# Two transformer blocks on one core: the program begins with the residual input, and four later pieces of its hand-written order are moved

## What is computed

```python
x = first_block(x, mem, ...)      # stage A: mlstm heads + memory attention (4 heads, 256 memory tokens), ffn
                                  # stage B: band attention (12 heads) + memory attention, ffn, rmsnorm
x = second_block(x, ...)          # stage C: 4 differential heads + 8 forgetting heads, ffn, rmsnorm

h = rmsnorm(x, norm_mix_g[0])
q, k, v, o, gates, q_mem = split(h @ a_w_in)          # q, k: causal conv over 4 tokens, then silu
mk, mv = split(mem @ mem_w_kv[0])                     # mem does not depend on x
mem_out = softmax(q_mem @ mk.T / 8) @ mv
x = x + concat([mix_out, mem_out]) @ w_out            # in each stage; then the ffn
...
od = rmsnorm_2(p @ v, subln_g) * 0.8                  # differential heads of stage C
```

## Time and profile before

| | |
|---|---|
| median of 3 runs | 1838.75 us |
| profiled execution, its own time | 1836.94 us |
| its span, first to last instruction | 1835.2 us |
| PE busy | 1815.8 us, 99% |
| DVE, ACT, POOL busy | 935.6, 726.6, 272.4 us |
| granted TensorE clock | 0.997 of full |
| moved by DMA | 173.43 MB, 95 GB/s on average |

### The profile page before, as it was taken

One profiled execution on the slowest core, in us unless ns is written; L12 is line 12 of the kernel. 1 busy time (PEld: TensorE's weight loads), 2 busy tenths in 40 slices (PEclk: granted clock), 3 DMA queues, 4 the chain that ended last, 5 costly groups with the idle time before them and its releaser, 6 DMA issues.

```text
span 1835.2 us, 21592 instructions
## 1 busy us (share of the span) xinstructions
PE 1815.8 (99%) x8853; PEld 1482.8 (81%) x8853; DVE 935.6 (51%) x1445; ACT 726.6 (40%) x1159; POOL 272.4 (15%) x241
## 2 busy tenths in 40 slices
PE   9999999999999999999999999999999999999998
PEld 7877788888888887787888888888876788888886
DVE  6877455442444456546543354458666443323324
ACT  5644444331332435654433133333566332222223
POOL 2001322210121200002221022003001222101210
PEclk9999999999999999999999999999999999999999
DMA  6121123222222332212222222232131223222221
GB/s 241 69 94 56 69 92 115 92 92 95 89 102 88 124 135 92 81 46 93 97 110 92 98 99 97 75 127 91 60 104 51 76 92 109 98 92 92 97 92 63
DMA packets 32338, 173.43 MB, mean 95 GB/s; under 512 B 4064, under 2 KB 6240, under 8 KB 14320
## 3 DMA queue, kind: packets, MB, share of 16 engines
q1 hardware_dynamic: 26848, 162.55, 24.7%
q10 hardware_dynamic: 5392, 9.51, 1.7%
HBM read 169.38 MB, written 2.13 MB: 93 GB/s over the span
## 4 chain that ended last, share of the span: by engine, by line
PE 93%; DVE 3%; ACT 2%; issue 0%; DMA 0%; POOL 0%; SPq 0%; ACTq 0%; DVEq 0%; POOLq 0%
PE ps L964 53%; PE ps L1239 19%; PE ps L898 7%; PE ps L983 6%; PE ps L1088 2%; PE ps L1133 2%; PE ps L1113 2%; DVE WL L1740 1%; PE ps L1172 1%; PE ps L1153 1%; DMA raw<-in_wall 0%; ACT PC L1476 0%; ACT WH L1315 0%; DVE hL L1708 0%; PE ps L878 0%
## 5 line engine op out<-in xcount | busy, mean ns | idle before, releaser
L964 PE MATMUL ps<-hH,WH 128*128 128x512 f32 x1456 | 571.4, 392 | 0.1
L964 PE MATMUL ps<-hH,WL 128*128 128x512 f32 x1456 | 566.8, 389 | 0.0
L964 PE MATMUL ps<-hL,WH 128*128 128x512 f32 x1456 | 566.7, 389 | 0.0
L1740 DVE TENSOR_TENSOR WL<-raw,WH 128x1024 fp32r<-128x1024 f32 (+2 forms) x308 | 377.3, 1264 | 352.0 <-ACT WH L1315 352.0
L1315 ACT ACTIVATE WH<-raw 128x1024 fp32r<-128x1024 f32 (+2 forms) x308 | 301.3, 1026 | 291.5 <-PE ps L1239 228.6
L964 PEld LDWEIGHTS ps<-hH,WH 128*128 128x128 f32 x1456 | 273.3, 188 | 64.4 <-issue 7.5
L964 PEld LDWEIGHTS ps<-hL,WH 128*128 128x128 f32 x1456 | 273.4, 188 | 57.4 <-issue 1.2
L964 PEld LDWEIGHTS ps<-hH,WL 128*128 128x128 f32 x1456 | 273.3, 188 | 57.1
L1239 PE MATMUL ps<-fL,WH 128*128 128x512 f32 x531 | 205.9, 388 | 0.0
L1239 PE MATMUL ps<-fH,WH 128*128 128x512 f32 x531 | 205.9, 388 | 0.0
L1239 PE MATMUL ps<-fH,WL 128*128 128x512 f32 x531 | 205.9, 388 | 0.0
(11 more groups left out here) (364 smaller groups left out, 1965.8 us busy)
## 6 DMA issues: line engine op xcount, KB each, us to landing
raw<-in_wall SPq DMA_DIRECT2D x140, 1024.0 KB, 4.6
raw<-in_wall SPq DMA_DIRECT2D x12, 768.0 KB, 4.0
bias<-in_bias ACTq DMA_DIRECT2D x12, 256.0 KB, 3.0
X<-in_xt SPq DMA_DIRECT2D x8, 256.0 KB, 9.1
CB<-rows ACTq DMA_DIRECT2D x8, 256.0 KB, 3.3
raw<-in_wall SPq DMA_DIRECT2D x4, 256.0 KB, 5.8
mrA<-in_memt ACTq DMA_DIRECT2D x4, 256.0 KB, 6.2
Mb<-m_rows ACTq DMA_DIRECT2D x4, 256.0 KB, 4.7
```

The lines of the kernel that those rows point to most:

```text
L964: mm = e.matmul(ps[b][:, 0:N], ww[:, k, c:c + 128], x[:, k, 0:N], start=(k == 0 and i == 0), stop=(k == 7 and i == 2))
L1740: e.tensor_tensor(WL[n % NCV][:, c], raw[n % NRAW][:, c], WH[n % NCV][:, c].bitcast(F32), ALU.subtract).then_inc(*mark("wl", n, x))
```

## The change

Five edits to the order, and nothing in what is computed:

1. **The start.** The unit of the memory's queries (3080 in `a_w_in`) becomes unit 0, the two memory units 1 and 2. X is loaded by ACT's queue as its first eight instructions (before: by SP, behind unit 1), the memory by SP behind unit 1 (before: by ACT); the constants K come behind them. `qm_first` takes the place of `mk_first`: 48 matmuls of 512 columns for 48 of 256, and keeps its two banks (`hold`) until the spread of the norm's factor. `mkA`, `mvA` and the gate products follow. The squares stand ahead of the memory's products and so ahead of the conversion of unit 3 (q), which stood ahead of them. The norm's two PE steps come after the first and the second tile of q (before: after the queries' second tile and the first tile of q), and one tile more (k, first) stands ahead of the first scores; every later step of stage A stands one tile later against the products.
2. **Drains at the first Rsb.** The gate's drain comes behind those of the queries; before it came first.
3. **Seventh parts.** `out_mid` runs for all four open tiles before the first `out_rest`, in stages A, B and C.
4. **The inverse.** `od_all` keeps DVE's reciprocal alone and stands right behind `probs` of pair 6; ACT's root is the new step `od_root` at the old place.
5. **The store** of four tiles of the first half is cut in two.

```diff
-    u = [("mem_w_kv", 0, 0, 8, 0, 256), ("mem_w_kv", 0, 0, 8, 256, 256)]
-    u += [("a_w_in", 0, 0, 8, 3080, 256)]
+    u = [("a_w_in", 0, 0, 8, 3080, 256)]
+    u += [("mem_w_kv", 0, 0, 8, 0, 256), ("mem_w_kv", 0, 0, 8, 256, 256)]
...
-STORES = ((0, 0, 2), (0, 2, 2), (0, 4, 4), (1, 0, 4), (1, 4, 2), (1, 6, 2))
+STORES = ((0, 0, 2), (0, 2, 2), (0, 4, 2), (0, 6, 2), (1, 0, 4), (1, 4, 2), (1, 6, 2))
...
-        for x in (0, 1):
+        for x in range(4):
             put("out_mid", stage, x, *opened[x])
...
-    for x in range(4):
-        put("conv", 0, x)
-        put("mem_part", "A", x)
-    now["conv"] = 1
-    take()
-    put("mk_first", 0)
+    for k in range(8):
+        if k % 2 == 0:
+            put("conv", 0, k // 2)
+        put("scaled", "mix0", k, None)
+    now["conv"], now["unit"] = 1, 1
+    put("qm_first", 0)
     done.add(0)
-    for m in range(2):
-        tile_done("mkcp", "mkA", m)
+    put("conv", 1, 0)
+    put("mem_part", "A", 0)
+    put("mem_part", "A", 1)
+    put("conv", 1, 1)
+    put("mem_part", "A", 2)
+    put("mem_part", "A", 3)
+    now["conv"] = 2
     put("gate_weights", "A")
-    for k in range(8):
-        put("scaled", "mix0", k, None)
-    tm(1, "memA", "mvA", "mvcp", ntt=2)
-    conv_ahead(4)
+    conv_ahead(3)
     for k in range(8):
         put("square", "s", k, "dve", "pool" if k % 2 else "act")
-    rstd("mix0", 60)
+    fm(1, "memA", "mkA", "mkcp", N=256)
+    tm(1, "memA", "mvA", "mvcp", ntt=2)
+    conv_ahead(5)
     put("gate_products", "A")
-    waiting.append(("gate",))
-    fm(1, "mix0", "qmA", "R")
+    norms.extend([("rstd_first", "mix0", 60), ("rstd_second", "mix0")])
+    waiting.extend([("R", "qmA", 0), ("R", "qmA", 1), ("gate",)])
...
-    fill(gens, 1)
+    fill(gens, 2)
...
-    after_values = {(5, 1): [("od_two",)], (6, 0): [("od_all",)], (6, 1): [("od_mask",)],
+    after_values = {(5, 1): [("od_two",)], (6, 0): [("od_root",)], (6, 1): [("od_mask",)],
...
+    def inverse(p):
+        if p == 6:
+            put("od_all")
...
+                    if a[0] == "mix0":
+                        turns.extend([BANK[("qmA", 0)], BANK[("qmA", 1)]])
...
-                        out_part(stage, b, n, c, seq[7 if m < 2 else early:], ("out", stage, m))
+                        out_part(stage, b, n, c, seq[7:], ("out", stage, m))
...
-                    src = memt.rearrange("p (k t) -> p k t", k=8)
-                    for i in range(4):
-                        e.dma_start(mrA[:, 2 * i:2 * i + 2, :], src[:, 2 * i:2 * i + 2, :]).then_inc(s_mem[i], 16)
+                    src = xt.rearrange("p (k t) -> p k t", k=8)
+                    for k in range(8):
+                        e.dma_start(X[:, k, :], src[:, k, :]).then_inc(s_x[k], 16)
```

More of the change, by code:

```diff
@@ L268, in mem_kv, with soft @@
         tm(1, "mem" + name, "mv" + name, "mvcp", ntt=2)
-    def soft(stage, gens, per, before=None, between=None):
+    def soft(stage, gens, per, before=None, between=None, after_probs=None):
         us = SOFT[stage]
@@ L286, in soft @@
                     put("probs", stage, p, x)
+            if after_probs:
+                after_probs(p)
             if early:
@@ L523, in order @@
     soft("C", gens, lambda p: {4: (1, 0), 5: (1, 0), 6: (1, 0), 7: (1, 0), 8: (1, 1), 9: (1, 1)}.get(p, (1, 1)),
-         None, between_C)
+         None, between_C, inverse)
     out_rest("C", "n2")
@@ L908, in tensor @@
                         e.matmul(ps[b][:, 0:256], diag[:, 0:128], diag[:, 0:256], start=True, stop=True)
-                elif what == "mk_first":
+                elif what == "qm_first":
                     n = a[0]
@@ L915, in tensor @@
                     W = [x[0][:, :].rearrange("p (k c) -> p k c", k=8) for x in (WH, WL)]
-                    bs = [bank(("mkA", m), ("mkv", "mkA", m))[0] for m in (0, 1)]
+                    bs = [bank(("qmA", m), ("linR", "qmA", m), hold=True)[0] for m in (0, 1)]
                     for k in range(8):
-                        if k in (2, 4, 6):
+                        if k == 2:
                             mm = e.matmul(ps[idle][:, 0:256], diag[:, 0:128], diag[:, 0:256], start=True, stop=True)
-                        if k == 6:
                             mm.then_inc(*mark("warmed"))
                         w.wait_ge(*at(*weights_at(n, k)))
-                        for x in act_at("memA", k):
+                        for x in normed("mix0", k):
                             w.wait_ge(*at(*x))
                         for m in (0, 1):
-                            for i, (ww, x) in enumerate(((W[0], mHA), (W[0], mLA), (W[1], mHA))):
-                                mm = e.matmul(ps[bs[m]][:, 0:256], ww[:, k, 128 * m:128 * m + 128], x[:, k, :],
+                            for i, (ww, x) in enumerate(((W[0], hH), (W[0], hL), (W[1], hH))):
+                                mm = e.matmul(ps[bs[m]][:, :], ww[:, k, 128 * m:128 * m + 128], x[:, k, :],
                                               start=(k == 0 and i == 0), stop=(k == 7 and i == 2))
                             if k == 7:
-                                mm.then_inc(*mark("lin", "mkA", m))
-                    FREED[n] = ("lin", "mkA", 1)
+                                mm.then_inc(*mark("lin", "qmA", m))
+                    FREED[n] = ("lin", "qmA", 1)
                 elif what == "gate_products":
@@ L1677, in scalar @@
                         *mark("odc", hd))
-                elif what == "od_all":
+                elif what == "od_root":
                     w.wait_ge(*at("odD", "r"))
@@ L1755, in vector @@
                         w.wait_ge(s_cols if ev.sems else None, 16)
-                        w.wait_ge(s_K if ev.sems else None, 16)
                         w.wait_ge(s_x[k] if ev.sems else None, 16)
@@ L1769, in vector @@
                     w.wait_ge(*at("rsq", a[0]))
+                    w.wait_ge(s_K if ev.sems else None, 16)
                     for x in RCOL_USED[a[0]]:
@@ L2382, in sync @@
                 e.dma_start(raw[0][:, 512 * x:512 * x + 512], wall[:, 512 * x:512 * x + 512]).then_inc(s_first[x], 16)
-            e.dma_start(cols[:, :], colsd).then_inc(s_cols, 16)
+                if x == 0:
+                    e.dma_start(cols[:, :], colsd).then_inc(s_cols, 16)
+            load(1)
+            src = memt.rearrange("p (k t) -> p k t", k=8)
+            for i in range(4):
+                e.dma_start(mrA[:, 2 * i:2 * i + 2, :], src[:, 2 * i:2 * i + 2, :]).then_inc(s_mem[i], 16)
             e.dma_start(K[:, :, :], consts.rearrange("p (i c) -> p i c", i=5)).then_inc(s_K, 16)
@@ L2386, in sync @@
             e.dma_start(graw[:, :, :], gatew[:, 0:64].rearrange("p (k c) -> p k c", k=8)).then_inc(s_gw, 16)
[L2387 to L2390, removed]
             for n in range(2, len(UNITS)):
```

## The result

The changed kernel takes 1846.58 us in the median (5 runs, 1843.04 to 1848.32) against 1837.82 us (5 runs, 1837.62 to 1839.1) for the kernel before: ratio 1.0044, interval 1.0033 to 1.0054. It is 8.8 us slower; 1843.0 was predicted, as 4.25 us more than the kernel before. The executions also lie 5.3 us apart, where those of before lie 1.5 apart. They follow the granted clock, taken as the mean over an execution: 1843.04 us at 0.998, 1844.92 at 0.996, 1846.58 at 0.995, 1848.18 and 1848.32 at 0.994.

A forecast was written before the change was run, and what follows sets the result against it. PE, busy 1815.8 of 1835.2 us, was taken as the bound. Terms -2.0 + 2.65 + 2.2 - 0.5 + 4.9 - 2.7 - 0.3 = +4.25 gave 1841.2 profiled, 1843.0 against the median; range 1838.0 to 1847.0.

The forecast's parts named there:

- Seventh parts: At `out_all` in A, B, C: mid parts moved ahead leave fewer products covering the conversion chain; PE waits longer, +4.9 us.
- The first k behind the spread: At the first k tile: PE stands still until DVE's queries' drains and `O` free the gates' bank, +2.65 us.
- The start: From launch to stage A's first scores: PE starts at 8.15, DVE's work around the squares decides, point reached earlier, -2.0 us.
- The memory heads' first values: Before the memory heads' values in stage A: DVE's copy PTA is late and PE waits, +2.2 us (0 to +2.9).
- mlstm's norm: At mlstm's norm: PE's 0.5 us wait for `fac` goes as DVE has less ahead, -0.5 us (-0.6 to 0).
- The inverse: Before pair 7's scores: reciprocal moves into DVE's pause, root and copies start earlier, PE's wait falls 3.61 to 0.9, -2.7 us.
- The store: In the last traffic: fuller transfer slices after cutting the four-tile store in two, -0.3 us (-0.5 to +0.1).
- DVE's delay runs on: Rival, stage A after the memory heads' values: drains stay 3 us late, PE waits again at k or v tile; 1846, chance 0.10.

The follow-up runs named there:

- The kernel with its waits filled: The changed kernel with PE multiplying constants, results thrown away, in the waits at the memory's keys, first k tile and `out_all` in A, B, C: 1843.31 us.
- the last experiment: The kernel before with the reciprocal's new place and only the first tile's mid part ahead of the first rest part: 1831.55 us, ratio 0.9966.
- the kernel with PE 4 us earlier: The changed kernel with the gate's drain put ahead of the queries' drains again, as before the change: 1846.18 us.

## Why the prediction was right and wrong

The direction was right, and the time lay in the stated range, 0.4 us below its upper end of 1847.0; it lay above the forecast's own range, which ended at 1845.0. The median is 3.6 us above the 1843.0, but the change itself was sized at half: +4.25 us forecast, +8.8 measured. That the times are only 3.6 apart and the changes 4.5 comes from the base: 1838.75 us was the median of three executions of before, and five give 1837.82. The kernel with its waits filled, which shows about what the change costs when the clock doesn't fall, takes 1843.31 us. That looks like the sum, but it is luck in part, since terms in it were off both ways:

- **Seventh parts** (+4.9): the waits are 2.31, 2.23 and 2.22 us where 2.35 was worked out for each, and the chain through add, hH, square and conversion is what binds. Shown by the edit alone and, in the other direction, by the last experiment. As a size the term failed: alone it costs 9.5 us, since each wait of 2.2 us can be followed by half clock that costs 1.6 us.
- **The first k behind the spread** (+2.65): 2.69 measured, and 1.48 with `O` first, where 1.45 was worked out. Another 1.65 us of half clock followed in the profile.
- **The start** (-2.0): wrong. The failed step is that the memory's keys and values follow the queries at 19.4 with no wait, and that what decides on DVE is only the work around the squares. PE began at 8.88, not 8.15, because hH and hL of the first tile stand ahead of it, ended the queries at 20.5, and waited 1.76 us for the memory's low part. I had counted DVE's work for the squares, and not the 6 us in which it does unit 1 and the memory behind X. The first tile of q started at 37.55, not 33.75. The wait of 0.85 at the first q tile, forecast for that work, didn't come since PE was later. At full clock the start is worth 0.0, with half clock behind the wait +1.8. (The sum to the gates' end has a slip: 19.4 + 5.7 + 5.7 + 1.9 is 32.7, not 32.9; the 33.75 doesn't hang on it.)
- **The memory heads' first values** (+2.2): 0.54. DVE's copy was late as worked out: with the first drain at 51.65 instead of 47.9 the sum's 104.95 becomes 108.7, and the values start at 108.86. PE's own time was off, by what the start and the clock had cost it. In the kernel with PE 4 us earlier the wait was 3.33. What is lost ahead of this point on PE counts little, as long as DVE is behind.
- **mlstm's norm** (-0.5): the wait of 0.5 us is gone; laid side by side the traces give -0.7.
- **The inverse** (-2.7): -5.3 alone. The wait fell to 0.30 us, not 0.9 (3.3 us), and the half clock behind it, 1.4 us, went. The wait is shorter than the 0.9 left over in the sum because ACT's copies PTC follow the root at once, 0.53 us behind its start (1404.24 and 1404.77); in before they began 1.12 us behind it (1392.83 and 1393.95), with two issues of transfers (1.07 us) from 1392.83 on, which in the changed kernel run from 1401.91, ahead of the root. The place and the table load's 1.28 us behaved as the row said. The further drain that the Trainium skill ("ScalarE: Activation LUTs", the section on what ACT_TABLE_LOAD costs) adds to a load isn't seen: the load starts at 1402.94 right behind ACT's previous instruction, and the root follows at 1404.24.
- **The store** (-0.3): not to be told from nothing.
- **Not in the sum at all**: 0.9 us in A's open tiles, which comes with the start: there DVE has four steps of the heads ahead of the low part that PE waits for.
- **The rivals**: 1846, the price of "DVE's delay runs on", is nearest to the median, but its sign isn't there. From PTA to the open output tiles at 238 PE waits nowhere 0.1 us or more.

So one mechanism was missing from the whole, the term that the prediction put at nothing: that PE's standing still has a second price behind it. It was in the trace of before, in the 3.42 us that twelve scores take in the earlier trace rows, a row that was quoted but read for its wait only. The parts measured alone add up to 9.5 - 5.3 + 6.4 + 0.8 = +11.4 against +8.8 for all. One reason for the difference can be seen: three of the four parts were measured in kernels that keep the wait before pair 7's scores, and the profiled executions of two of them have 6.8 us of half clock there, while the changed kernel has neither the wait nor that. The rest is within what the half clock does or doesn't do from one execution to the next; I can't assign it closer.

## What to carry to other kernels

When PE is busy 99% of the time, price a new wait of 2 us on it as a range from 2 to nearly 4, and a removed one too: look in the rows behind the old waits for products that take longer than their fellows, and in the spread of the executions for how often. When an order is changed to cover one wait, count the products that are left between the last thing the conversion chain waits for and its user; moving products ahead of the chain's start takes cover away one for one (here six products, 1.4 us, and three, 0.7 us, the other way). Before crediting an earlier PE, ask which engine sets the next meeting point: here DVE's copy at 108 us took back what PE had won.

## What the runs showed of the hardware

In the ten traces the granted clock, outside the first microseconds and the tail, left its upper level only around the end of a wait of PE. How often it did so went with the length of the wait, but not by it alone:

| wait of PE, us | places in the traces | followed by half clock |
|---|---|---|
| 1.48 to 1.77 | 7 | 1 |
| 2.22 to 2.32 | 12 | 7 |
| 2.69 | 3 | 3 |
| 3.33 to 3.83 | 5 | 5 |

Waits of the same length at the same place went both ways: behind 1.76 us at the start 0.57 over the window, behind 1.75 us at the same place in another kernel 1.00; behind 2.22 us in C 1.00, and behind 2.23 us there in another kernel 0.66. A stretch at the lower level lasted some 3 to 4 us, and 6.8 us in two of the traces, at the 3.74 and 3.80 us waits. With products of constants in the waits the granted clock was 1.00 at every place looked at. The scatter between executions goes with it: 0.9 us with the waits filled and 0.65 without the 3.61 us wait, against 5.3 and 2.1.
